# FFN input projections with stationary weights in a two-layer decoder trunk

## The reference

```python
def rms_norm(x, g):
    y = xf * lax.rsqrt(jnp.mean(xf * xf, axis=-1, keepdims=True) + EPS)
    return (y * g).astype(x.dtype)

def swiglu(h, w_in, w_out):                 # w_in 1024 x 5632, w_out 2816 x 1024
    a, b = jnp.split(h @ w_in, 2, axis=-1)
    return (jax.nn.silu(a) * b) @ w_out

x = x + 0.5 * swiglu(rms_norm(x, norm_g[l, 0]), ffn_w_in[l, 0], ffn_w_out[l, 0])
```

## Time and profile before

| | |
|---|---|
| median of 3 runs | 1064.94 us (1064.58 to 1068.81) |
| the profiled execution | 1067.82 us, of which the span is 1065.8 us |
| TensorE busy | 1046.3 us, 98% of the span, 5156 matmuls and transposes |
| VectorE busy | 598.0 us, 56% |
| ScalarE busy | 525.9 us, 49% |
| mean DMA rate | 171 GB/s |
| mean granted TensorE clock | 0.988 of full |

### The profile page before, as it was taken

The page is one execution under the profiler, slowest core; times in us unless marked ns, Lnnn a source line. Parts: engine busy times, 40 slices in busy tenths (PEclk is TensorE's granted clock), DMA queues, the critical chain, the costliest instruction groups (busy, mean ns, idle before and its releaser), DMA issues.

```text
span 1065.8 us, 14153 instructions
## 1 busy us (share of the span) xinstructions
PE 1046.3 (98%) x5156; PEld 870.7 (82%) x5156; DVE 598.0 (56%) x833; ACT 525.9 (49%) x692; POOL 73.4 (7%) x108
## 2 busy tenths in 40 slices
PE   8999999999999999999999999999998999999997
PEld 7888888888888888888888888888887888888886
DVE  5545545777475564445567775445565556555444
ACT  7433444656475554433455543443465646334444
POOL 0040000000013000000000390000000000000000
PEclk9999999999899999999999999999999999999999
DMA  7685756457201365555544665555544136555541
GB/s 248 228 228 188 242 180 223 160 178 242 93 2 41 118 198 197 191 167 193 198 156 160 237 197 197 197 177 188 187 158 158 41 108 213 187 185 194 197 158 40
DMA packets 128709, 182.45 MB, mean 171 GB/s; under 512 B 5960, under 2 KB 100272, under 8 KB 128544
## 3 DMA queue, kind: packets, MB, share of 16 engines
q1 hardware_dynamic: 127040, 176.18, 49.8%
q0 software_dynamic: 1456, 5.72, 2.4%
q10 hardware_dynamic: 176, 0.05, 0.0%
HBM read 180.34 MB, written 1.59 MB: 171 GB/s over the span
## 4 chain that ended last, share of the span: by engine, by line
PE 95%; DVE 2%; ACT 1%; issue 1%; DMA 0%; ACTq 0%; DVEq 0%
PE inb L405 15%; PE inb L403 15%; PE inb L404 15%; PE acc L403 13%; PE acc L405 13%; PE acc L404 13%; PE inb L640 2%; PE tb L512 2%; PE acc L613 2%; PE tb L625 2%; PE inb L637 1%; PE tb L592 1%; DVE work L1461 1%; PE acc L397 0%; PE tb L397 0%
## 5 line engine op out<-in xcount | busy, mean ns | idle before, releaser
L1321 DVE TENSOR_TENSOR wlo<-raw,whi 128x2048 fp32r<-128x2048 f32 x108 | 250.1, 2316 | 233.7 <-ACT whi L927 233.7
L927 ACT CAST whi<-raw 128x2048 fp32r<-128x2048 f32 x108 | 206.5, 1912 | 217.3 <-PE acc L405 117.8
L403 PE MATMUL inb<-whi,thi 128*128 128x512 f32 x720 | 281.7, 391 | 0.0
L405 PE MATMUL inb<-whi,tlo 128*128 128x512 f32 x720 | 280.5, 390 | 0.0
L404 PE MATMUL inb<-wlo,thi 128*128 128x512 f32 x720 | 280.2, 389 | 0.0
L405 PEld LDWEIGHTS inb<-whi,tlo 128*128 128x128 f32 x720 | 135.2, 188 | 28.5
L404 PEld LDWEIGHTS inb<-wlo,thi 128*128 128x128 f32 x720 | 135.2, 188 | 27.9
L403 PEld LDWEIGHTS inb<-whi,thi 128*128 128x128 f32 x720 | 135.2, 188 | 27.8
L1304 DVE TENSOR_TENSOR wlo<-raw,whi 128x2048 fp32r<-128x2048 f32 x55 | 128.7, 2344 | 47.1 <-ACT whi L914 46.9
L403 PE MATMUL acc<-whi,ghi 128*128 128x512 f32 x320 | 128.5, 402 | 0.0
L405 PE MATMUL acc<-whi,glo 128*128 128x512 f32 x320 | 125.1, 391 | 0.0
(11 more groups left out here) (231 smaller groups left out, 988.0 us busy)
## 6 DMA issues: line engine op xcount, KB each, us to landing
raw<-in_ffn_w_in SPq DMA_DIRECT2D x174, 512.0 KB, 4.8
raw<-in_ffn_w_out SPq DMA_DIRECT2D x88, 512.0 KB, 4.0
raw<-in_nsa_w_in SPq DMA_DIRECT2D x20, 512.0 KB, 4.2
raw<-in_fox_w_kvf SPq DMA_DIRECT2D x16, 512.0 KB, 4.3
raw<-in_nsa_cmp_w SPq DMA_DIRECT2D x8, 512.0 KB, 4.8
raw<-in_nsa_w_out SPq DMA_DIRECT2D x8, 512.0 KB, 4.5
raw<-in_fox_w_q SPq DMA_DIRECT2D x8, 512.0 KB, 4.4
raw<-in_fox_w_out SPq DMA_DIRECT2D x8, 512.0 KB, 4.6
```

The lines of the kernel that those rows point to most:

```text
L403: pe.matmul(o, lh, rh, start=start, stop=False, skip_group_check=True)
L405: return pe.matmul(o, ll, rh, start=False, stop=stop, skip_group_check=True)
L927: act.copy(whi[u % RING][:, :], raw[u % RING][:, :]).then_inc(s_hi, 1)
L1321: dve.tensor_tensor(wlo[u % RING][:, :], raw[u % RING][:, :], whi[u % RING][:, :].bitcast(F32), ALU.subtract).then_inc(s_lo, 1)
```

## The change

In chunks 1 to 10 of every FFN the operands of the input projection change places. A 128x128 block of weights is stationary. Tokens stream: the rounded tokens and the remainders lie side by side in one buffer `th` (k-tile, rounded or remainder, 256 tokens), so one 512-column matmul with `whi` gives two of the three products in the two halves of a bank, and one 256-column matmul with `wlo` adds the third into the first half. A unit is 4 column blocks (m) x 4 k-tiles x 2 = 32 matmuls. Four banks (`inb[0]`, `inb[1]`, `tb[0]`, `tb[1]`) hold the four blocks, hidden columns on partitions: a in the first two, b in the others. VectorE adds the two halves of each bank (`summed`), multiplies a by a row of 1/rms by token (`silu_input`), and forms the product (`hidden_product`); no transposes follow. The factor 1/rms of b moves into the residual add. The row of 1/rms comes from two small matmuls per FFN (`rstd_rows`). Chunk 0 stays as it was, except that its transposes go to bank `acc[2]`. In the last chunk the order by token tile falls away.

```diff
-        thi = sb("thi", [P, KT, SEQ], F32R)
-        tlo = sb("tlo", [P, KT, SEQ], F32R)
+        th = sb("th", [P, KT, 2, SEQ], F32R)
+        thi, tlo = th[:, :, 0, :], th[:, :, 1, :]
+        mbanks = [inb[0], inb[1], tb[0], tb[1]]
...
+            def rstd_rows(name):
+                pe.wait_ge(s_rstd, NORMS.index(name) + 1)
+                for t in range(NT):
+                    mm = pe.matmul(acc[3][:, t * P:(t + 1) * P], rstd[:, t:t + 1].broadcast_to([P, P]),
+                                   ident[:, :], start=True, stop=True)
+                mm.then_inc(s_rrow, 1)
+
+            def unit_turned(slot, half, need, banks_free=None):
+                pe.wait_ge(s_lo, need)
+                if banks_free is not None:
+                    pe.wait_ge(s_sum, banks_free)
+                for m in range(4):
+                    for k in range(4):
+                        kk = 4 * half + k
+                        col = slice(k * CW + m * P, k * CW + (m + 1) * P)
+                        pe.matmul(mbanks[m][:, :], whi[slot][:, col], th[:, kk].rearrange("p x n -> p (x n)"),
+                                  start=kk == 0, stop=False, skip_group_check=True)
+                        mm = pe.matmul(mbanks[m][:, 0:SEQ], wlo[slot][:, col], th[:, kk, 0, :],
+                                       start=False, stop=kk == KT - 1, skip_group_check=True)
+                    if half == 1 and m < 3:
+                        mm.then_inc(s_in, 1)
+                mm.then_inc(s_used, 1)
...
                 with pe.Fori(2, NJ - 1) as j:
-                    for half in range(2):
-                        u = b + 2 + half
-                        unit_in(u % RING, half, inb, 3 * (j - 1) + u + 1)
+                    unit_turned((b + 2) % RING, 0, 3 * (j - 1) + b + 3, 4 * (j - 1) + c0)
+                    unit_turned((b + 3) % RING, 1, 3 * (j - 1) + b + 4)
                     pe.wait_ge(s_lo, 3 * (j - 1) + b + 5)
                     pe.wait_ge(s_glo, j + h0)
                     out_part(slot, 0, 0)
                     out_part(slot, 0, 1)
                     out_part(slot, 1, 0)
-                    hidden_turn(2 * j + 2 * n0 + 2)
                     out_part(slot, 1, 1).then_inc(s_used, 1)
...
+                unit_turned(u % RING, 0, u + 1, 4 * (NJ - 2) + c0)
+                unit_turned((u + 1) % RING, 1, u + 2)
                 pe.wait_ge(s_lo, u + 3)
+                pe.wait_ge(s_glo, h0 + NJ - 1)
                 out_part((u + 2) % RING, 0, 0)
                 out_part((u + 2) % RING, 0, 1)
+                out_part((u + 2) % RING, 1, 0)
                 pe.wait_ge(s_lo, u + 4)
                 pe.wait_ge(s_glo, h0 + NJ)
                 out_last((u + 3) % RING, 0)
-                hidden_turn(2 * (n0 + NJ), [1])
-                out_part((u + 2) % RING, 1, 0)
-                pe.wait_ge(s_glo, h0 + NJ + 1)
+                out_part((u + 2) % RING, 1, 1).then_inc(s_used, 1)
                 if following:
                     turn(following, 0)
-                out_part((u + 2) % RING, 1, 1).then_inc(s_used, 1)
                 out_last((u + 3) % RING, 1)
```

On VectorE (the scalar engine's new order is: cast, silu of 512 elements, cast, copy of the product to `ghi`, cast):

```diff
+            def summed(m):
+                dst = (sa if m < 2 else gg)[:, m % 2, :]
+                dve.tensor_reduce(dst, mbanks[m][:, :].rearrange("p (x n) -> p n x", x=2), AX.X,
+                                  ALU.add).then_inc(s_sum, 1)
...
                 with dve.Fori(1, NJ - 1) as j:
-                    hidden_lo(j + h0)
+                    dve.wait_ge(s_in, 3 * (j - 1) + m0 + 1)
+                    summed(0)
                     lo_loop(b + 5, j)
-                    hidden(2 * j + 2 * n0)
+                    dve.wait_ge(s_in, 3 * (j - 1) + m0 + 2)
+                    summed(1)
+                    silu_input(4 * (j - 1) + c0 + 2)
+                    dve.wait_ge(s_in, 3 * (j - 1) + m0 + 3)
+                    summed(2)
+                    dve.wait_ge(s_used, 3 * (j - 1) + b + 4)
+                    summed(3)
+                    hidden_product(j + n0 + 2, 4 * (j - 1) + c0 + 4)
                     lo_loop(b + 6, j)
+                    hidden_lo(j + h0 + 1, ghi[:, :, :], glo[:, :, :])
                     lo_loop(b + 7, j)
```

More of the change, by code:

```diff
@@ L236, in yoco_trunk @@
         s_silu = sem("silu_done")
+        s_in = sem("in_columns")
+        s_sum = sem("in_columns_summed")
+        s_ar = sem("silu_input")
+        s_rrow = sem("rstd_row_turned")
+        s_rc = sem("rstd_row_copied")
         s_g = sem("hidden_ready")
@@ L964, in o_hi @@
                 act.wait_ge(s_ot, first + g + 1)
-                act.copy(thi[:, 2 * g:2 * g + 2, :].rearrange("p k n -> p (k n)"),
-                         inb[1][:, :]).then_inc(s_ohi, 1)
+                act.copy(thi[:, 2 * g:2 * g + 2, :],
+                         inb[1][:, :].rearrange("p (k n) -> p k n", k=2)).then_inc(s_ohi, 1)
             def boundary(name, u):
@@ L980, in silu_tile, with silu_turned, hidden_turned_hi, hidden_hi @@
                 act.activation(sa[:, t, :], banks[t][:, 0:FC], ACT.Silu, scale=rstd[:, t:t + 1]).then_inc(s_silu, 1)
[L982 to L987, removed]
-                act.wait_ge(s_gt, n)
[L989 to L995, removed]
+            def silu_turned(n):
+                act.wait_ge(s_ar, n)
+                act.activation(sa[:, :, :], sa[:, :, :], ACT.Silu).then_inc(s_silu, 1)
+            def hidden_turned_hi(n):
+                act.wait_ge(s_gt, n)
+                act.copy(ghi[:, :, :].rearrange("p k n -> p (k n)"), acc[2][:, :]).then_inc(s_ghi, 1)
+            def hidden_hi(n, dst):
+                act.wait_ge(s_g, n)
+                act.copy(dst.rearrange("p k n -> p (k n)"),
+                         gg[:, :, :].rearrange("p k n -> p (k n)")).then_inc(s_ghi, 1)
             def ffn(f):
-                b, h0 = U_FFN[f], (NJ + 1) * f
-                act.wait_ge(s_in0, 2 * f + 1)
+                b, a0, g0 = U_FFN[f], (NJ - 1) * f, (NJ + 1) * f
+                act.wait_ge(s_in0, f + 1)
                 silu_tile(0, acc)
@@ L1363, in boundary, with hidden_tile @@
                 root(name)
-            def hidden_tile(n, t, banks=inb):
+            def hidden_tile(n, t):
                 dve.wait_ge(s_silu, n + 1)
[L1368 to L1375, removed]
+                dve.tensor_tensor(gg[:, t, :], acc[t][:, FC:2 * FC], sa[:, t, :], ALU.mult).then_inc(s_g, 1)
@@ new lines, in silu_input, with hidden_product, hidden_lo @@
+            def silu_input(n):
+                dve.wait_ge(s_sum, n)
+                dve.tensor_tensor(sa[:, :, :], sa[:, :, :], rstd_row[:, :].unsqueeze(1).broadcast_to([P, 2, SEQ]),
+                                  ALU.mult).then_inc(s_ar, 1)
+            def hidden_product(n, summed_n):
+                dve.wait_ge(s_sum, summed_n)
+                dve.wait_ge(s_silu, n)
+                dve.tensor_tensor(gg[:, :, :], gg[:, :, :], sa[:, :, :], ALU.mult).then_inc(s_g, 1)
+            def hidden_lo(n, hi_part, lo_part):
@@ L1390, in ffn @@
-                hidden(2 * n0, acc)
+                b, n0, h0, m0, c0 = U_FFN[f], (NJ + 1) * f, NJ * f, 3 * (NJ - 1) * f, 4 * (NJ - 1) * f
+                for t in range(NT):
+                    hidden_tile(n0 + t, t)
                 if f:
@@ L1393, in ffn @@
                 lo(b + 4)
+                hidden_turned_lo(h0 + 1)
+                dve.wait_ge(s_rrow, f + 1)
+                dve.tensor_copy(rstd_row[:, :], acc[3][:, 0:SEQ]).then_inc(s_rc, 1)
+                dve.wait_ge(s_rc, f + 1)
                 with dve.Fori(1, NJ - 1) as j:
-                    hidden_lo(j + h0)
+                    dve.wait_ge(s_in, 3 * (j - 1) + m0 + 1)
+                    summed(0)
                     lo_loop(b + 5, j)
-                    hidden(2 * j + 2 * n0)
+                    dve.wait_ge(s_in, 3 * (j - 1) + m0 + 2)
[6 more added lines that the diff above has]
+                    hidden_product(j + n0 + 2, 4 * (j - 1) + c0 + 4)
                     lo_loop(b + 6, j)
+                    hidden_lo(j + h0 + 1, ghi[:, :, :], glo[:, :, :])
                     lo_loop(b + 7, j)
[L1400 to L1403, removed]
+                dve.wait_ge(s_in, m0 + 3 * (NJ - 2) + 1)
+                summed(0)
                 lo(b + FFN_UNITS - 1)
-                hidden_tile(last + 1, 1)
+                dve.wait_ge(s_in, m0 + 3 * (NJ - 2) + 2)
+                summed(1)
+                silu_input(c0 + 4 * (NJ - 2) + 2)
+                dve.wait_ge(s_in, m0 + 3 * (NJ - 2) + 3)
+                summed(2)
+                dve.wait_ge(s_used, b + FFN_UNITS - 2)
+                summed(3)
+                hidden_product(n0 + NJ + 1, c0 + 4 * (NJ - 1))
+                hidden_lo(h0 + NJ, ghi_last, glo_last)
                 lo(b + FFN_UNITS)
                 ffn_add(f, 0)
-                hidden_last_lo(h0 + NJ + 1, 1)
             def ffn_add(f, t):
@@ L1417, in ffn_add @@
                     xc = xs[:, t, n * CW:(n + 1) * CW]
```

(2 more changed lines are left out.)

65 lines of the change are left out of this document (24 added, 41 removed).

## The result

The changed kernel takes 1068.99 us, median of 13 runs (1065.23 to 1070.05); the kernel before takes 1065.29 beside it. The ratio is 1.0028, 95% interval [1.0017, 1.0039]: slower by 0.3%, about 3.0 us by the ratio (3.7 between the medians), within the 0.5% that the prediction called no change, though a series of 13 runs does tell it from zero. A later series gave 1.0018 [1.0005, 1.0030]. The forecast was 1059, 6 us faster. The profiled execution took 1069.77 us, its span is 1067.8.

The account below looks back on a forecast made before the run. TensorE's instruction stream was taken as the bound (98% busy, 95% of the chain). Terms -19.6 + 9.0 + 1.6 + 1.8 + 0.6 + 0.5 = -6.1 us gave 1059 us on the median's scale, range 1048 to 1069.

Parts of the forecast that it names:

- the boundary: Start of the next stage, three times: turn of tile 0 slightly late behind VectorE's adds, +0.6 us (0 to 2).
- The couple at 347 ns: Rebuilt input units: a 512-column and a 256-column matmul take 227 + 120 ns, +9.0 us over 80 units.
- the transient: First few matmuls after a change of width are slow: 0.04 us a chunk, +1.6 us in all.
- rival 2's mild form: 512-column matmuls stay at 0.235 us: couple 356 ns, 1069 us; decides from 352 ns; chance 0.16 with the full form.
- Rival 2's full form: Every load behind a 256-column matmul is waited for: couple 415 ns, +87 us on the forecast, 1146 us; chance 0.04.
- the rule of the Trainium skill: Input units: loads overlap only across different row groups, so eight extra loads a unit cost +68 us; the prediction rejected it.
- The transposes: Chunks 1 to 10 of each FFN: transposes removed from TensorE's path, 0.49 us a group of four, -19.6 us in all.
- The row of 1/rms: Two small fp32 matmuls per FFN behind chunk 0's kept transposes: 0.45 us each time, +1.8 us in all.
- rival 3: VectorE ends last in chunk 10, with reduces at half speed (1.2 us): +4.9 us and +1 at boundaries, 1065 us; chance 0.16.
- the 0.65 forecast: VectorE's reduce adding the two halves of a bank takes 0.65 us, off the path in a steady chunk.
- The last chunk's hidden remainder: Last chunk of each FFN: VectorE ends it at 9.25 us, 0.4 us before TensorE needs it, so no stall.
- The end: Final norm after the last FFN: about 1.8 us less matmul cover, +0.5 us (0 to 1.2).

Follow-up runs that it names:

- widths_in_blocks: Changed kernel with widths changed twice a chunk: first unit 16 wide then 16 narrow matmuls, second unit 16 narrow then 16 wide; 1066.44 us, ratio 1.0007.
- all_wide: Changed kernel with the 256-column matmul streaming 512 columns too, adding the product of both remainders; 1193.41 us in one run.
- other_half: Changed kernel with the 256-column product written to the second half of its bank instead of the first; 1070.32 us in one run.
- across_banks: Changed kernel with widths still alternating, but no matmul writing the bank that the one before it wrote; 1083.37 us in one run.
- after_again: The changed kernel once more, unchanged, as base for two others on the same chip; 1068.43 us, ratio 1.0018 to the kernel before.

## Why the prediction was wrong

It named what bounds the kernel and the direction of each term, and missed the size of two: the couple, which alone turned the forecast gain into a small loss, and the boundary, where it also followed the wrong instruction.

*The couple at 347 ns failed.* The prediction took the nearest rows, one 512-column matmul behind a run of 256-column ones, read "the gaps settle after a few matmuls" and gave 1.6 us in all for the transient. Measured is 353 ns: 13 ns over 340, x 1280 = 16.6 us in place of 9.0, and about 2 us in the output products in place of 1.6. The premise that went wrong is that a stream settles although it changes width at every instruction. `widths_in_blocks` shows 227 + 120 when it may settle, `all_wide` shows no price for loads or operand roles, `other_half` and `across_banks` none for banks. So rival 2's mild form came true in its mechanism, and past its decision point of 352 ns. That its time, 1069, was also measured is partly luck: it stood for 356 ns, and 353 alone give +1.9 us; the other half came from the boundary, which that rival did not have. The second figure of the earlier trace rows, 0.24 us from 224.35 to 224.59, was the state in which every couple lives; I used it as a bound and should have weighed it as the likely case. Rival 2's full form, an uncovered load, is excluded. So is, in these traces, the rule of the Trainium skill that the prediction weighed ("TensorE: Matmul & The Clock Gate", Part 3, by which every load here would be exposed): `all_wide` hides 32 full loads a unit at 227 ns a matmul.

*The transposes were right.* -19.6 us forecast; 0.48 us a group measured in the loop, about -19.3 for all.

*The row of 1/rms was right*, at the low side. The turn of chunk 0 and the two fp32 matmuls behind it, on TensorE:

```profile
27.91 0.60 PE L520 MATMUL acc<-ident,gg 128*128 128x128 f32 x4
28.34 0.61 PE L527 MATMUL acc<-ident,rstd 128*128 128x128 f32 x4
28.71 0.48 PE L540 MATMUL inb<-th,whi 128*128 128x512 f32 x1
```

They take 28.71 - 28.34 = 0.37 us, 1.5 in all against 1.8.

*VectorE and rival 3.* The groups of instructions by form, beside the earlier trace rows:

```profile
L1391 DVE TENSOR_REDUCE sa<-inb 128x256 f32<-128x512 f32 x80 | 55.0, 687 | 78.7 <-PE inb L542 78.2 <-DVE rstd_row L1418 0.5
L1391 DVE TENSOR_REDUCE gg<-tb 128x256 f32<-128x512 f32 x80 | 51.2, 682 | 0.0
L1402 DVE TENSOR_TENSOR gg<-gg,sa 128x512 f32<-128x512 f32 x40 | 28.5, 712 | 4.6
```

A reduce takes 0.68 us though its two addends lie 1 KB apart in PSUM, near the 0.65 forecast and far from the 1.2 of rival 3. The last chunk's hidden remainder ended in time, and TensorE had no gap there in the changed kernel, as forecast. How thin that cover is, the reordered kernels showed: where the first bank filled later, a start came 1.3 us (`widths_in_blocks`) or 3.2 us (`across_banks`) after the one before in each last chunk.

*The boundary was under-sized.* Forecast +0.6; the gaps at the three stage starts behind an FFN are 0.75 us from start to start where the kernel before has 0.03: +2.2. A fourth, ahead of layer 2's first FFN, grew from 0.62 to 0.92, which makes +2.5; but it is 0.67 in `after_again` and runs from 0.28 to 1.12 over the other traces, so its 0.3 can't be put down to the change. I followed the chain to tile 0's split tokens, found that it fits, and stopped; the instruction queued behind it on VectorE, the remainder of the second weight unit, was late next.

*The end*: +0.5 forecast. From the first output product of the last FFN's chunk 9 to the end, the span went from 17.33 to 17.64 us, though the split turns (0.5 us) had gone: +0.8, within its range.

The sum with measured terms is -19.3 + 16.6 + 2.0 + 1.5 + 2.5 + 0.8 = +4.1 us. Measured are 3.0 by the ratio, 3.7 between the medians and 2.1 between the two spans, unrounded. By stages the traces agree with the sum. The lengths and busy times of the four FFNs, each to the next stage's first matmul, before and after:

```profile
sum 751.26, PE 744.85 PEld 615.35 DVE 400.59 ACT 343.87 POOL 53.61; mean PE 186.21 PEld 153.84 DVE 100.15 ACT 85.97 POOL 13.40
```

```profile
sum 755.09, PE 746.73 PEld 633.60 DVE 524.41 ACT 338.10 POOL 50.47; mean PE 186.68 PEld 158.40 DVE 131.10 ACT 84.53 POOL 12.62
```

They take 3.8 us longer, and the stage ahead of the fourth gap 0.3. What hides half of it in the spans is the second mixer, before and after (its window and length, busy time by engine, granted clock, DMA share and GB/s):

```profile
794.10:877.36 83.26, 78.13 (x451) 66.42 (x450) 46.63 (x131) 47.32 (x94) 0.57 (x1) 0.94 0.33 108
```

```profile
797.69:878.69 81.00, 74.95 (x449) 63.59 (x449) 46.63 (x132) 46.48 (x92) 0.57 (x1) 0.98 0.34 111
```

It is 2.3 us shorter at a granted clock of 0.98 in place of 0.94: TensorE was at 1.2 GHz for 3.4 us of it in place of 10.2. In the 13 traces of this case the mixer takes 83.1 to 83.3 us with 10.2 us at that level, 81.4 to 81.5 with 6.8 and 79.9 to 81.1 with 3.4, and so its length goes with the clock, whichever kernel runs (the group of 10.2 us has both kernels that keep the old projection and two that have the new one). Whether the change has a part in where the clock falls is not shown.

## What to carry to other kernels

Cost a matmul stream by its start-to-start times in the very pattern it will have: a place where two patterns meet shows the transient, and the pattern that alternated here never left it. Before two spans are compared, look at the granted clock stage by stage: each 3.4 us at 1.2 GHz was worth about 1 us here where TensorE was busy. When matmuls of two widths must mix, group them by width as far as the consumers of their banks allow, and keep bank-by-bank order only where a consumer is nearly late. And when a chain moves on an in-order engine, follow it past the first consumer to what is queued behind it.

## What the hardware did that was not expected

- Start-to-start times of a 512-column fp32r matmul are 227 ns in a settled stream and mostly 229 to 236 ns (with a 224 now and then) for two to nine matmuls after transposes or narrower ones (the first one after transposes takes 314). Strict alternation with 256-column ones holds them at 236.2 on average, in a pattern of 236, 233 and 241 that repeats every three couples (1.06 us), whatever bank or half is written. Why is open.
- 256-column ones sit at 120 ns in a long run and at 113 to 120 when alternating: the whole loss lies on the wide matmul.
- A 128x128 load behind each matmul is hidden at both widths: 1280 narrow matmuls were followed by the next start after 113 to 120 ns, though a load is recorded with 188.
- At the end of three of the four waits of 2.8 us in `across_banks` the granted clock fell to 0.50 for 3.4 us, and at the end of the fourth it did not.
